# Four edits in a hybrid mixer and mixture-of-experts kernel: score blocks in pairs, logits in 32-token groups, an early subtraction, and a new home for the last down weights

## The chip, the cores and the metric

The kernel runs on one core of one Trainium2 chip. The metric is the time of one execution on the device, in microseconds (us); lower is better. All times below are of single executions or of medians of them.

## What is computed

One layer of a streaming encoder over 1024 prompt tokens and 64 sample tokens, all in float32. Cut to what matters:

```
h = rms_norm(x) * (1 + sc1) + sh1
hq, hf, hi, hog, gq, gk, gv, gog, glr, ga, gb = split(h @ w_in)      # one combined input projection
o_hg  = chunked gated linear attention, 4 heads of dk 128, decay from hf        # "hg" units
log_g = log_sigmoid(glr @ w_gk2 + b_gk) / 16                                     # low-rank gate
o_gla = chunked gated linear attention, 4 heads of dk 64, decay log_g           # "gla" units
merged = sigmoid(ga) * (o_hg @ w_br_a) + sigmoid(gb) * (o_gla @ w_br_b)
x = x + g1 * (merged @ w_out)
h = rms_norm(x) * (1 + sc2) + sh2
group = top1(h @ w_rg + b_rg); experts = top2 of 8 in the group (h @ w_re + b_re)   # 4 + 32 = 36 logits a token
x = x + g2 * sum over the two experts of wts * (silu(h @ w_gate[e]) * (h @ w_up[e])) @ w_down[e]
y = rms_norm(x)
```

There are 32 experts with gate and up weights of 1024 x 512 and down weights of 512 x 1024.

## The kernel before, in words

Matrix products in float32 precision are made as three products of operands split into a rounded half ("hi", the engine's fast float32 form) and a rest ("lo"): `split_matmul`, lines 149 to 151. The hi half is a copy to the rounded type (on GpSimd for the projection weights, line 737; on ScalarE for the experts' weights, line 2406). The lo half is a VectorE subtraction (line 1466 in the mixers, called `next_low`; line 2528 in the experts, called `low`). Small products (attention scores, outputs, transposes, logits) run as plain float32 matmuls, of which the trace records two passes each, every pass with a weight load of its own.

Each engine runs its own instruction list in program order; semaphores (`reach`, `wait_ge`) tie the lists together. So what comes late on one engine delays all that stands behind it on that engine.

**Mixers.** Six units run one after the other: two gla units of two heads (units 0 and 1), then four hg units of one head (units 2 to 5). The tokens are 9 tiles, eight of 128 and one of 64. In each unit TensorE first makes the unit's projections (`project`, three column chunks of 364, 364 and 360 tokens, 24 matmuls each), then runs the loop over `j`, one step for a tile and head: 18 steps in a gla unit, 9 in an hg unit. Step `j` makes the transposes of a new tile (`turn`, lines 804 and 806, when a tile begins), the score blocks of the next step (`scores(u, j + 1)`, line 820), projections of the next unit where some are due (`filled`; in a gla unit in every even step, in an hg unit in steps 0, 1, 3, 4, 6 and 7, in the last unit in steps 0 to 2), and the outputs of this step (`outputs(u, j)`, lines 847, 849 and 851). `scores` makes 28 products for a tile of 128: 24 of 32 tokens by 32 tokens, four blocks of 32 output partitions in turn, and 4 "far" ones; the array is used 32 output columns at a time. VectorE turns scores into a masked matrix with four instructions (`mask`, lines 1430 to 1440) and then advances the state (`advance`, line 1453). There are two score buffers: `scores(u, j)` waits until `mask` of `j - 2` has ended (`sc_ready`). `outputs(u, j)` needs `mask(j)`, the transposed tile that ScalarE copies (`keep_tok`, line 1139), and the state after `j - 1`.

**Start of unit 0.** After the channel products TensorE makes the low-rank product, its logits, the projection `q` and then `x0`, for which the lo half of the third weight block is needed (`w_lo_done` 3). VectorE makes that half in the loop over the seven levels, after the third level (`if l == 2: next_low()`). Before the levels it has `decay_log(0)`, `decay_bound(0)` and `decay_sum(0)`, which wait for three ScalarE steps. ScalarE's list holds the copy of `q` chunk 1 behind the exponentials of levels 0 and 1 (line 1080), and `project` of `x0` chunk 0 waits for that copy, too (`proj_kept`).

**Output projection and router.** For each tile `t` TensorE transposes `h2` (line 2058), makes half of the output projection of tile `t + 2`, then the logits of tile `t` (line 2069: for each of 8 channel blocks one matmul with 128 tokens as weights and 36 columns), then the other half. Tiles 7 and 8 have no projection behind them; there the routing of the last tiles is a chain of small VectorE instructions.

**Experts.** For each expert: `gate_up` (48 matmuls), transposes of the next expert's tokens, `down` of the expert before (24 matmuls), transposes of the hidden values. The raw weights arrive in a ring of eight 1 MB buffers. Behind the loop stands `down(NE - 1)` for the last expert. ScalarE's list at the last expert (31) is: the silu steps, `keep_y(30)` (copy of the result, which waits for `down(30)`), `hidden_high(31)`, the two halves of `high("d", 31)`. VectorE's is: `hidden(31)`, `hidden_low(31)`, the two halves of `low("d", 31)`. The split down weights go to `d_hi` and `d_lo`, which are in use until `down(30)` has ended. `down` starts when `hidden_low` and the first `low("d")` have ended.

Of the kernel before, what the change touches and what calls it, by code (L numbers as in the profile page):

```python
# [27 lines left out]
F32 = mybir.dt.float32  # L28
# [463 lines left out]
def mixers(nc, a, h, h_hi, h_lo, m_hi, m_lo, merged, ident, mod_d, mix_d, gate_d, outs, consts, ahead):  # L492
# [66 lines left out]
    with Stage(nc, "x") as s:  # L559
# [207 lines left out]
        def _(pe):  # L767
# [190 lines left out]
            for u in range(NU):  # L958
# [18 lines left out]
                for j in range(NS[u]):  # L977
                    if j + 1 < NS[u]:
                        if (j + 1) % SUB[u] == 0:
                            turn(u, (j + 1) // SUB[u])  # L980
                        scores(u, j + 1)
                    for (of, name), c in filled(u, j):
                        project(of, name, c)
                    outputs(u, j)
# [349 lines left out]
        def _(dve):  # L1334
# [202 lines left out]
            V.memset(p_far, 0.0).then_inc(far_zero, 1)  # L1537
            V.memset(state[:, :, :, :], 0.0).then_inc(state_zero, 1)
            decay_log(0)
            decay_bound(0)  # L1540
            decay_sum(0)
            for u in range(NU):
# [4 lines left out]
                for l in range(NL):  # L1547
                    level_diff(u, l)
                    if l == 2:
                        next_low()  # L1550
                    if l == 3:
                        ends_diff(u)
# [129 lines left out]
def out_router(nc, a, mod_d, x2_d, h2_d, m_hi, m_lo, ident, consts, route, early, ahead):  # L1682


    NTT = NT + 1
    eid, pos, wts, m_all = route["eid"], route["pos"], route["wts"], route["m_all"]
    with Stage(nc, "o") as s:
# [349 lines left out]
        def tensor(pe):  # L2037
# [23 lines left out]
            def logits(t):  # L2061
                n = TILES[t][1]
                reach(pe, hT_ready, t + 1)
                if t:
                    reach(pe, logits_kept, t)
                else:
                    pe.wait_ge(small_in, 64)
                for k in range(KD):
                    m = nc.tensor.matmul(p_l[0:n, 0:36], hT[:, k, 0:n], w_r[:, k, :], start=(k == 0), stop=(k == KD - 1))  # L2069
                m.then_inc(logits_done, 1)  # L2070
# [58 lines left out]
NE = 32  # L2129
# [33 lines left out]
def experts(nc, a, mod_d, x2_d, outs, consts, route, table_d, h2_d, y_d, ident, early, router):  # L2163
# [6 lines left out]
    with Stage(nc, "e") as s:  # L2170
# [82 lines left out]
        his, los, used = {"g": g_hi, "u": u_hi, "d": d_hi}, {"g": g_lo, "u": u_lo, "d": d_lo}, {"g": g_done, "u": u_done, "d": d_done}  # L2253

        def staged(part, e, half):

            return weight_rows(w[place[part, e, half] % RING], part)
# [138 lines left out]
        def _(act):  # L2396
            router.scalar(act)

            def high(part, e, halves=(0, 1)):

                for half in halves:
                    i = place[part, e, half]
                    reach(act, w_in[i % RING], 16 * (i // RING + 1))
                    if e and half == 0:
                        reach(act, used[part], e)
                    nc.scalar.activation(his[part][:, half_rows(part, half), :], staged(part, e, half), ACT.Copy).then_inc(hi_done[part], 1)  # L2406

# [36 lines left out]
            for e in range(NE):  # L2444
# [5 lines left out]
                if e:  # L2450
                    keep_y(e - 1)
                hidden_high(e)
                high("d", e)
            keep_y(NE - 1)
# [50 lines left out]
        def _(dve):  # L2505
# [17 lines left out]
            def low(part, e, halves=(0, 1)):  # L2523

                for half in halves:
                    rows = half_rows(part, half)
                    reach(dve, hi_done[part], 2 * e + half + 1)
                    V.tensor_tensor(los[part][:, rows, :], staged(part, e, half), his[part][:, rows, :].bitcast(F32),  # L2528
                                    ALU.subtract).then_inc(lo_done[part], 1)
# [72 lines left out]
            for e in range(NE):  # L2602
                hidden(e)
                if e + 1 < NE:
                    low("g", e + 1, (1,))
                    x_low(e + 1)
                    low("u", e + 1)
                hidden_low(e)
                low("d", e)
            n = number(dve)  # L2610
# [54 lines left out]
        def _(pe):  # L2665
# [33 lines left out]
            def down(e):  # L2699
# [9 lines left out]
                m.then_inc(d_done, 1)  # L2709

            router.tensor(pe)
            pe.wait_ge(filled, 2)
# [3 lines left out]
            for e in range(NE):  # L2716
# [5 lines left out]
                turn_hidden(e)  # L2722
            down(NE - 1)
            n = number(pe)
# [132 lines left out]
```

## Time and profile before

| | us |
|---|---|
| median of 3 runs | 1673.09 (1672.48 to 1675.18) |
| the profiled execution, its own time | 1672.9 |
| span of its trace | 1670.8 |
| TensorE busy | 1561.6 (93%) |
| TensorE weight loads busy | 1368.7 (82%) |
| VectorE busy | 1196.5 (72%) |
| ScalarE busy | 921.7 (55%) |
| GpSimd busy | 298.3 (18%) |

"PE" is TensorE's matmuls, "PEld" its weight loads, "DVE" VectorE, "ACT" ScalarE, "POOL" GpSimd; L820 is line 820 of the kernel. A busy TensorE is not one at its peak: matmuls are pipelined and the recorded duration of one reaches over the start of the next. So what a matmul costs is read from the distance between starts, not from durations. "Granted clock" is the share of full clock that TensorE was given.

### The profile page before, as it was taken

Reading aid. Unit: us, or ns where it says so; the run is one execution under the profiler, and the core shown is the slowest. Engines: PE = TensorE matmul, PEld = TensorE weight load, DVE = VectorE, ACT = ScalarE, POOL = GpSimd, SP = SyncE. Lnnn points to the kernel's source line nnn. Section 1 sums busy time; section 2 is a strip of 40 time slices with the busy share of each in tenths; the row PEclk is TensorE's granted clock in tenths of the full one; section 3 lists DMA queues with packets and bytes.
Section 4 is the critical chain, followed back from the end, with each engine's and each line's share of the span. In section 5 each row is a group of like instructions: output and inputs, shape, how many; then the busy total and the mean of one; then the engine's idle time right before and its main releaser. Section 6 shows DMA issues by size and latency. Waiting matters only on the chain. (4 is left out here: it accounts for less than half of the span.)

```text
span 1670.8 us, 29394 instructions
## 1 busy us (share of the span) xinstructions
PE 1561.6 (93%) x12436; PEld 1368.7 (82%) x12436; DVE 1196.5 (72%) x1537; ACT 921.7 (55%) x1094; POOL 298.3 (18%) x203
## 2 busy tenths in 40 slices
PE   5999999999999999998998995999999999999956
PEld 4899899999889989897997874788888888888842
DVE  5743583368466675758565467999999999999937
ACT  5542444336353463633112223888888888888832
POOL 2310020002010010102000001132344342232230
PEclk9999999999999999998999996999999999999988
DMA  9121022111324152324446338999999999999965
GB/s 332 49 78 34 23 69 93 40 42 43 118 74 150 58 189 89 96 96 139 152 159 220 118 115 311 341 373 386 392 383 394 386 380 388 383 381 396 373 221 227
DMA packets 129660, 346.07 MB, mean 207 GB/s; under 512 B 16464, under 2 KB 72504, under 8 KB 103864
## 3 DMA queue, kind: packets, MB, share of 16 engines
q1 hardware_dynamic: 113704, 312.29, 51.7%
q0 software_dynamic: 9824, 17.88, 2.8%
q10 hardware_dynamic: 6000, 13.99, 2.2%
q8 instruction: 100, 1.64, 0.4%
q14 instruction: 32, 0.26, 0.0%
HBM read 316.04 MB, written 43.81 MB: 215 GB/s over the span
## 5 line engine op out<-in xcount | busy, mean ns | idle before, releaser
L149 PE MATMUL wo_psum_m<-h_hi,x_w_hi 128*128 128x364 f32 (+1 forms) x1184 | 404.4, 342 | 9.7 <-DVE x_w_lo L1466 2.9
L151 PE MATMUL wo_psum_m<-h_hi,x_w_lo 128*128 128x364 f32 (+1 forms) x1184 | 390.4, 330 | 0.0
L150 PE MATMUL wo_psum_m<-h_lo,x_w_hi 128*128 128x364 f32 (+1 forms) x1184 | 390.4, 330 | 0.0
L149 PEld LDWEIGHTS wo_psum_m<-h_hi,x_w_hi 128*128 128x128 f32 x1184 | 223.7, 189 | 25.1 <-issue 12.8
L150 PEld LDWEIGHTS wo_psum_m<-h_lo,x_w_hi 128*128 128x128 f32 x1184 | 224.0, 189 | 2.5
L151 PEld LDWEIGHTS wo_psum_m<-h_hi,x_w_lo 128*128 128x128 f32 x1184 | 223.8, 189 | 0.0
L737 POOL CAST x_w_hi<-x_w 128x1024 fp32r<-128x1024 f32 x44 | 70.1, 1593 | 617.7 <-PE wo_psum_m L151 597.4
L2315 POOL DMA_INDIRECT scratch_y<-e_y,all_tbl x32 | 74.2, 2320 | 372.8 <-ACT e_y L2439 372.8
L1466 DVE TENSOR_TENSOR x_w_lo<-x_w,x_w_hi 128x1024 fp32r<-128x1024 f32 x52 | 65.2, 1253 | 92.5 <-POOL x_w_hi L737 61.7
L149 PE MATMUL e_psum_y<-e_d_hi,e_hid_hi 128*128 128x512 f32 x256 | 103.1, 403 | 5.3 <-DVE e_d_lo L2528 5.3
L149 PE MATMUL e_psum_g<-e_g_hi,e_x_hi 128*128 128x512 f32 x256 | 104.9, 410 | 3.2 <-DVE e_x_lo L2539 2.6
L151 PE MATMUL e_psum_g<-e_g_hi,e_x_lo 128*128 128x512 f32 x256 | 101.6, 397 | 0.0
L150 PE MATMUL e_psum_g<-e_g_lo,e_x_hi 128*128 128x512 f32 x256 | 101.4, 396 | 0.0
L151 PE MATMUL e_psum_y<-e_d_hi,e_hid_lo 128*128 128x512 f32 x256 | 100.3, 392 | 0.0
L150 PE MATMUL e_psum_y<-e_d_lo,e_hid_hi 128*128 128x512 f32 x256 | 100.2, 392 | 0.0
L151 PE MATMUL e_psum_u<-e_u_hi,e_x_lo 128*128 128x512 f32 x256 | 99.8, 390 | 0.0
L149 PE MATMUL e_psum_u<-e_u_hi,e_x_hi 128*128 128x512 f32 x256 | 99.6, 389 | 0.0
L150 PE MATMUL e_psum_u<-e_u_lo,e_x_hi 128*128 128x512 f32 x256 | 99.6, 389 | 0.0
L1035 ACT ACTIVATE x_x<-wo_psum_m 128x364 f32<-128x364 f32 (+1 forms) x48 | 22.5, 469 | 121.7 <-PE wo_psum_m L151 121.6
L1430 DVE TENSOR_TENSOR x_diag<-wo_psum_m,all_shapes 128x192 f32<-128x192 f32 (+1 forms) x72 | 37.1, 516 | 68.0 <-PE wo_psum_m L820 67.4
L2528 DVE TENSOR_TENSOR e_g_lo<-mg_ring_hi,e_g_hi 128x2048 fp32r<-128x2048 f32 x34 | 77.7, 2289 | 9.7 <-ACT e_g_hi L2406 9.5
L2528 DVE TENSOR_TENSOR e_d_lo<-mg_ring_lo,e_d_hi 128x2048 fp32r<-128x2048 f32 x34 | 76.2, 2284 | 1.1 <-ACT e_d_hi L2406 1.1
(380 smaller groups left out, 3521.6 us busy)
## 6 DMA issues: line engine op xcount, KB each, us to landing
mg_ring_hi<-in_w_e_gate SPq DMA_DIRECT2D x34, 1024.0 KB, 9.8
mg_ring_lo<-in_w_e_down SPq DMA_DIRECT2D x34, 1024.0 KB, 8.3
mg_ring_hi<-in_w_e_up SPq DMA_DIRECT2D x32, 1024.0 KB, 8.8
mg_ring_lo<-in_w_e_up SPq DMA_DIRECT2D x32, 1024.0 KB, 8.7
mg_ring_lo<-in_w_e_gate SPq DMA_DIRECT2D x30, 1024.0 KB, 9.9
mg_ring_hi<-in_w_e_down SPq DMA_DIRECT2D x30, 1024.0 KB, 8.1
x_w<-in_w_in SPq DMA_DIRECT2D x44, 512.0 KB, 3.9
scratch_gate<-x_x ACTq DMA_DIRECT2D x16, 544.0 KB, 3.3
```

The source lines that it names most:

```text
L149: nc.tensor.matmul(out, lhs[0], rhs[0], start=start, stop=False)
L150: nc.tensor.matmul(out, lhs[0], rhs[1], start=False, stop=False)
L151: return nc.tensor.matmul(out, lhs[1], rhs[0], start=False, stop=stop)
L737: nc.gpsimd.tensor_copy(w_hi[:, n % 2], w[:, n % 2]).then_inc(w_hi_done, 1)
L1035: nc.scalar.activation(dst[:, c0:c0 + n], bank[:, 0:n], ACT.Copy).then_inc(proj_kept, 1)
L1430: V.tensor_tensor(diag[0:n, j % 2].rearrange("p t l -> p l t"), p_diag[0:n, j % 2].rearrange("p (l t) -> p l t", t=SB), masks[0:n], ALU.mu ...
L1466: V.tensor_tensor(w_lo[:, n % 2], w[:, n % 2], w_hi[:, n % 2].bitcast(F32), ALU.subtract).then_inc(w_lo_done, 1)
L2315: nc.gpsimd.indirect_dma_start(out=y_d, out_offset=bass.IndirectOffsetOnAxis(ap=tbl[:, e:e + 1], axis=0), in_=y[:, e % 2, :], in_offset=No ...
L2528: V.tensor_tensor(los[part][:, rows, :], staged(part, e, half), his[part][:, rows, :].bitcast(F32), ALU.subtract).then_inc(lo_done[part], 1)
```

## The change

It does four things.

1. In the loop over `j`, the score blocks of steps `j + 1` and `j + 2` are both issued in even steps, and none in odd steps. Nothing is added or removed.
2. Each logits matmul becomes four (two for the tile of 64 tokens), each for 32 tokens, written to 32 output partitions.
3. In unit 0 the third `next_low()` stands ahead of `decay_log(0)` instead of behind the third level. (It is the lo half of a weight block; the low-rank product itself isn't moved.)
4. The last expert's down weights are split into the buffers of the gate weights. ScalarE's and VectorE's lists at expert 31 are reordered: first half of the down weights, hidden values, second half. `down(31)` becomes `last_down`, which issues the same 48 products in another order: all hi x hi first, then hidden hi with the lo of the first half, then hidden lo with all hi, then hidden hi with the lo of the second half.

```diff
@@ mixers, TensorE, loop over j
                     if j + 1 < NS[u]:
                         if (j + 1) % SUB[u] == 0:
                             turn(u, (j + 1) // SUB[u])
-                        scores(u, j + 1)
+                    for ahead_ in (1, 2):
+                        if j % 2 == 0 and j + ahead_ < NS[u]:
+                            scores(u, j + ahead_)
                     for (of, name), c in filled(u, j):
                         project(of, name, c)
                     outputs(u, j)
@@ mixers, VectorE
             V.memset(state[:, :, :, :], 0.0).then_inc(state_zero, 1)
+            next_low()
             decay_log(0)
...
                     level_diff(u, l)
-                    if l == 2:
+                    if l == 2 and u:
                         next_low()
@@ router, TensorE
                 for k in range(KD):
-                    m = nc.tensor.matmul(p_l[0:n, 0:36], hT[:, k, 0:n], w_r[:, k, :], start=(k == 0), stop=(k == KD - 1))
+                    for b0 in range(0, n, SPAN):
+                        m = nc.tensor.matmul(p_l[b0:b0 + SPAN, 0:36], hT[:, k, b0:b0 + SPAN], w_r[:, k, :],
+                                             start=(k == 0), stop=(k == KD - 1))
@@ experts, where the split halves go
+        def split_into(part, e):
+
+            if part == "d" and e == NE - 1:
+                return g_hi[:, :, :].rearrange("p (f h) c -> p f (h c)", f=KF), g_lo[:, :, :].rearrange("p (f h) c -> p f (h c)", f=KF)
+            return his[part], los[part]
@@ experts, ScalarE
-                    if e and half == 0:
+                    if part == "d" and e == NE - 1:
+                        reach(act, g_done, NE)
+                    elif e and half == 0:
                         reach(act, used[part], e)
...
                 if e:
                     keep_y(e - 1)
-                hidden_high(e)
-                high("d", e)
+                if e + 1 < NE:
+                    hidden_high(e)
+                    high("d", e)
+            high("d", NE - 1, (0,))
+            hidden_high(NE - 1)
+            high("d", NE - 1, (1,))
             keep_y(NE - 1)
@@ experts, VectorE
-                hidden_low(e)
-                low("d", e)
+                if e + 1 < NE:
+                    hidden_low(e)
+                    low("d", e)
+            low("d", NE - 1, (0,))
+            hidden_low(NE - 1)
+            low("d", NE - 1, (1,))
@@ experts, TensorE
+            def last_down():
+
+                e = NE - 1
+                hi, lo = split_into("d", e)
+                halves = [range(half * KF // 2, (half + 1) * KF // 2) for half in range(2)]
+                reach(pe, y_kept, e)
+                reach(pe, h_hi_done, e + 1)
+                for half, fs in enumerate(halves):
+                    reach(pe, hi_done["d"], 2 * e + half + 1)
+                    for c in range(0, D, HALF):
+                        for f in fs:
+                            nc.tensor.matmul(p_y[0:N, c:c + HALF], hid_hi[:, f, :], hi[:, f, c:c + HALF], start=(f == 0), stop=False)
+                reach(pe, lo_done["d"], 2 * e + 1)
...
-            down(NE - 1)
+            last_down()
```

## Rows read from the trace of the kernel before

**Rows 1.** Busy time by stage: window, length, PE, PEld, DVE, ACT, POOL, clock, DMA, GB/s.
```profile
320.00:360.00 40.00, 40.00 (x816) 36.16 (x815) 28.48 (x67) 15.27 (x32) 2.09 (x2) 1.00 0.11 29
...
920.00:960.00 40.00, 40.00 (x214) 34.07 (x213) 17.39 (x24) 7.07 (x13) 0.00 (x0) 1.00 0.30 111
...
1400.00:1440.00 40.00, 40.00 (x190) 33.51 (x189) 38.29 (x26) 35.83 (x29) 9.84 (x4) 1.00 1.00 388
```

**Rows 2.** Timeline, start of unit 0: start, length, engine, line, [idle before, releaser].
```profile
59.47 1.04 POOL L737 CAST x_w_hi<-x_w 128x1024 fp32r<-128x1024 f32 x1 [2.28 <-PE wo_psum_m L151]
...
68.47 1.29 DVE L1339 SCALAR_TENSOR_TENSOR x_t<-x_b,x_t 128x1088 f32<-128x1088 f32 x1 [7.28 <-ACT x_t L1049]
...
77.11 0.46 ACT L1033 ACTIVATE x_q<-wo_psum_m 128x364 f32<-128x364 f32 x1
...
77.24 2.06 DVE L1466 TENSOR_TENSOR x_w_lo<-x_w,x_w_hi 128x1024 fp32r<-128x1024 f32 x1
...
79.44 0.41 PE L149 MATMUL wo_psum_m<-h_hi,x_w_hi 128*128 128x364 f32 x1 [2.88 <-DVE x_w_lo L1466]
```

**Rows 3.** Busy time behind the stall of rows 2; columns as in rows 1.
```profile
79.40:83.50 4.10, 4.06 (x15) 4.09 (x16) 4.10 (x7) 1.83 (x3) 0.00 (x0) 0.58 0.47 128
```

**Rows 4.** Timeline, TensorE, one score block between a transpose and a projection.
```profile
556.15 0.27 PE L806 MATMUL x_psum_tok<-all_ident,x_v 128*128 128x128 f32 x1
556.36 0.27 PE L820 MATMUL wo_psum_m<-x_q,x_k 128*32 128x32 f32 x8
556.44 0.68 PE L820 MATMUL wo_psum_m<-x_lev 128*32 128x32 f32 x48
557.05 0.43 PE L149 MATMUL wo_psum_m<-h_hi,x_w_hi 128*128 128x364 f32 x1
```

**Rows 5.** Timeline, step 0 of units 1 and 2: mask 0 and score block 1.
```profile
313.17 0.52 DVE L1430 TENSOR_TENSOR x_diag<-wo_psum_m,all_shapes 128x192 f32<-128x192 f32 x1 [1.60 <-PE wo_psum_m L820]
...
313.63 0.67 PE L820 MATMUL wo_psum_m<-x_lev 64*32 64x32 f32 x48
...
314.44 0.29 DVE L1440 TENSOR_TENSOR x_sc<-x_sc,wo_psum_m 128x128 f32<-128x128 f32 x1
...
437.81 0.64 PE L820 MATMUL wo_psum_m<-x_lev 128*32 128x32 f32 x43
...
439.47 0.29 DVE L1440 TENSOR_TENSOR x_sc<-x_sc,wo_psum_m 128x128 f32<-128x128 f32 x1
```

**Rows 6.** Timeline, TensorE, unit 3: the transpose of step 6, and outputs behind outputs.
```profile
564.38 0.33 PE L804 MATMUL x_psum_tok<-all_ident,x_ke 128*128 128x128 f32 x1 [0.62 <-ACT x_tok L1139]
...
576.59 0.41 PE L847 MATMUL x_psum_o<-x_qe,x_state 128*128 128x64 f32 x2 [0.59 <-issue]
```

**Rows 7.** Timeline, router: the logits of one tile, what follows, and of the last tile.
```profile
990.48 1.87 PE L2069 MATMUL o_psum_l<-o_w_r,o_hT 128*128 128x36 f32 x16
...
992.18 0.43 PE L149 MATMUL wo_psum_m<-x_out,mg_hi 128*64 128x512 f32 x1
...
1010.84 0.19 DVE L1900 TENSOR_TENSOR wo_ring<-o_psum_l,o_b_r 64x36 f32<-64x36 f32 x1 [0.90 <-PE o_psum_l L2069]
```

**Rows 8.** Timeline, last expert, from the end of down(30) to the last product.
```profile
1600.13 1.02 ACT L2439 ACTIVATE e_y<-e_psum_y 128x1024 f32<-128x1024 f32 x1 [7.25 <-PE e_psum_y L151]
1601.05 0.59 ACT L2433 ACTIVATE e_hid_hi<-e_psum_h 128x512 fp32r<-128x512 f32 x1
...
1603.32 1.91 ACT L2406 ACTIVATE e_d_hi<-mg_ring_lo 128x2048 fp32r<-128x2048 f32 x1
...
1605.67 2.29 DVE L2528 TENSOR_TENSOR e_d_lo<-mg_ring_lo,e_d_hi 128x2048 fp32r<-128x2048 f32 x1
1605.91 0.77 PE L149 MATMUL e_psum_y<-e_d_hi,e_hid_hi 128*128 128x512 f32 x1 [5.35 <-DVE e_d_lo L2528]
...
1612.42 0.39 PE L150 MATMUL e_psum_y<-e_d_lo,e_hid_hi 128*128 128x512 f32 x1
1612.65 0.39 PE L151 MATMUL e_psum_y<-e_d_hi,e_hid_lo 128*128 128x512 f32 x1
```

More of the change, by code:

```diff
@@ L1682, in out_router @@
 def out_router(nc, a, mod_d, x2_d, h2_d, m_hi, m_lo, ident, consts, route, early, ahead):
-    NTT = NT + 1
+    NTT, SPAN = NT + 1, 32
     eid, pos, wts, m_all = route["eid"], route["pos"], route["wts"], route["m_all"]
@@ L2403, in high @@
                     reach(act, w_in[i % RING], 16 * (i // RING + 1))
-                    if e and half == 0:
+                    if part == "d" and e == NE - 1:
+                        reach(act, g_done, NE)
+                    elif e and half == 0:
                         reach(act, used[part], e)
-                    nc.scalar.activation(his[part][:, half_rows(part, half), :], staged(part, e, half), ACT.Copy).then_inc(hi_done[part], 1)
+                    nc.scalar.activation(split_into(part, e)[0][:, half_rows(part, half), :], staged(part, e, half), ACT.Copy).then_inc(hi_done[part], 1)
             def x_high(e):
@@ L2527, in low @@
                     reach(dve, hi_done[part], 2 * e + half + 1)
-                    V.tensor_tensor(los[part][:, rows, :], staged(part, e, half), his[part][:, rows, :].bitcast(F32),
+                    if part == "d" and e == NE - 1:
+                        dve.wait_ge(g_done, NE)
+                    hi, lo = split_into(part, e)
+                    V.tensor_tensor(lo[:, rows, :], staged(part, e, half), hi[:, rows, :].bitcast(F32),
                                     ALU.subtract).then_inc(lo_done[part], 1)
@@ L2709, in down @@
                 m.then_inc(d_done, 1)
+            def last_down():
[10 more added lines that the diff above has]
+                reach(pe, lo_done["d"], 2 * e + 1)
+                for c in range(0, D, HALF):
+                    for f in halves[0]:
+                        nc.tensor.matmul(p_y[0:N, c:c + HALF], hid_hi[:, f, :], lo[:, f, c:c + HALF], start=False, stop=False)
+                reach(pe, h_lo_done, e + 1)
+                for c in range(0, D, HALF):
+                    for f in range(KF):
+                        nc.tensor.matmul(p_y[0:N, c:c + HALF], hid_lo[:, f, :], hi[:, f, c:c + HALF], start=False, stop=False)
+                reach(pe, lo_done["d"], 2 * e + 2)
+                for c in range(0, D, HALF):
+                    for f in halves[1]:
+                        m = nc.tensor.matmul(p_y[0:N, c:c + HALF], hid_hi[:, f, :], lo[:, f, c:c + HALF], start=False, stop=(f == KF - 1))
+                m.then_inc(d_done, 1)
             router.tensor(pe)
```

## The prediction, made before the changed kernel was run

> **What bounds the kernel now.** I read busy time by stage first. In three windows far apart, in the mixers' loop, in the router and in the experts, TensorE is busy for all of 40 us at full granted clock [rows 1]. So in these stages an instruction taken out of TensorE's list comes off the time, unless a wait for another engine takes its place. In the experts the DMA engines stand at 1.00 as well, but the change takes no TensorE work out there except at the end. Second, the list of TensorE's idle times over 0.25 us: about 50, nearly all at the start of the kernel, at the turns between units, in the last routing and at the end. Two of them are touched by the change: 2.88 us at 79.44 for a lo half [rows 2] and 5.35 us at 1605.91 for another [rows 8]. Third, the timeline around score blocks, logits and these two waits, from which I take distances between starts.
>
> **Logits in 32-token groups.** Now: 16 weight-load-and-matmul pairs (8 matmuls, two passes each) from 990.48 to the next kind of work at 992.18 take 1.70 us, 0.106 us a pair [rows 7]. After: 64 pairs with 32 weight columns. The nearest rows are the scores, with the same 32 output columns in four groups in turn: 48 pairs last 0.68 us, of which about 0.20 is the last one's own duration, so (0.68 - 0.20) / 47 = 10.2 ns a pair [rows 4]. 64 pairs are 0.66 us. But such a block has fixed costs at both ends: its first pair comes 0.21 us after a transpose that, at full width, takes 0.11 (0.10 extra), the next work starts 0.11 us later than the pace gives (0.69 us from 556.36 to 557.05 for 56 pairs, 0.57 at the pace), and the first projection matmul lasts 0.43 us against 0.33 of its kind (0.10 more) [rows 4]. Sum 0.31 us. New block 0.97 us, gain 0.73 us for a tile. TensorE is the bound for tiles 0 to 6 (7 x 0.73 = 5.1). Tile 7's logits lie before a wait of TensorE for VectorE: nothing. Tile 8's: VectorE idles 0.90 us for them [rows 7]; it has two groups instead of four, so half the pairs at, I assume, twice the distance, the same 0.66 us and 0.31; 0.7 to 0.9 us go, I take the 0.9 of the idle time. What is late next there is VectorE's own list. Logits: **-6.0 us**. Bounds: 0.106 us a pair (no concurrency at all) would be 6.8 us a block, +5.4 a tile; a pace of 7 ns gives -0.2 more a tile. I take the scores' pace, since width, groups and kind are the same; 36 columns against 32 are the only difference.
>
> The Trainium skill, page "TensorE: Matmul & The Clock Gate", section "Wait — 56ns, not 53.3ns?", speaks against this edit: starts of matmuls never come closer than about 25 ns. By it 64 pairs would take 1.6 us and the block 1.9 us, more than now. The trace disagrees: 10.2 ns a pair in the scores [rows 4]. The skill's "TensorEngine Tiling (Array Packing)", section "Tiling Modes", says that changing the tiling mode drains the engine, while tiles of one mode run in parallel; the extra 0.31 us at the ends of a score block are what such a drain would look like.
>
> **Score blocks in pairs.** The block itself stays. Of the two blocks of a pair, one pair of ends goes: 0.31 us [rows 4]. Pairs: 8 in each gla unit (17 blocks behind the first), 4 in each hg unit, 32 in all: 32 x 0.31 = 9.9 us. Against that stand new waits:
> - The second block of a pair waits for `mask(j)`, whose scores came a pair earlier. In steps from 2 on the mask is made under the projections of the step before; costed at nothing, by 4 us of projections against two masks of 1.56 us (313.17 to 314.73) [rows 5]. In step 0 there is no such cover. Unit 1: block 1 ends at 313.63 + 0.68 - 0.1 = 314.2, mask 0 at 314.73, so block 2 starts about 0.6 us late [rows 5]; unit 0 has the same form, 0.6. Unit 2: block 1 ends at about 438.35, mask 0 at 439.76, since VectorE had a lo half in front of it: 1.5 us [rows 5]. Units 3 to 5: the transpose of tile 1 already waits for ScalarE, and mask 0 ends in that time: 0.
> - In hg units, outputs of odd steps without projections now stand directly behind outputs of the step before and need its state. One such place is in the trace: 0.59 us of idle time at 576.59 [rows 6]. With the transpose (0.22) between, 0.37 us for step 5 of each hg unit.
> - In step 6 the transpose waits for ScalarE until 564.38, 0.62 us [rows 6]. ScalarE comes no earlier, while TensorE has a block and its ends less in front of this wait: of the gain, 0.9 us less the 0.37 (counted once) is lost, 0.9 in all with it for units 2, 3 and 4.
>
> Sum: units 0 and 1 8 x 0.31 - 0.6 = 1.9 each; unit 2 1.24 - 1.5 - 0.9 = -1.2; units 3 and 4 1.24 - 0.9 = 0.35 each; unit 5, whose steps 3 to 8 have no projections, 1.24 - 0.37 = 0.9. **-4.2 us**. Bounds: -9.9 (no new wait) and +3 (a wait of 0.4 us in each pair).
>
> **The lo half ahead of the decay.** The half takes VectorE 2.06 us at 77.24, and TensorE waits 2.88 us for it [rows 2]. Its source is ready at 59.47 + 1.04 = 60.5, and VectorE is idle for 7.28 us before 68.47 [rows 2]: there it is free, its cover is that idle time, and without it it would cost 1.3 to 2.1. Late next is ScalarE's copy of `q` chunk 1, 77.11 + 0.46 = 77.57 [rows 2], whose releasers (levels 0 and 1) don't move. So TensorE starts at about 77.65 instead of 79.44: 1.8 us. After the stall the granted clock was 0.58 for 4.1 us, 15 matmuls in 4.1 us; at full clock these are 2.5 [rows 3]. The clock was full before this stall. With 1.1 us of idle time left I expect that it stays so, as it did through the 0.62 us at 564.38 [rows 6]; at 1.1 us no row here shows it. 1.6 us. **-3.4 us**; bounds -1.8 (the clock falls all the same) and -4.5.
>
> **The last down weights.** The gate buffers are free early, but ScalarE's `keep_y(30)` stands in front of the first split and ends with `down(30)`, at 1600.13 + 1.02 [rows 8]. So the split starts no earlier than the list allows: the new home buys nothing by itself, the order does. After: first hi half from 1601.05 (where `hidden_high` was), 1.80 us; `hidden_high` 1602.85 to 1603.44; second hi half to 1605.2. TensorE starts at 1603.5 instead of 1605.91. It then idled for 3.0 us and will run at half clock for about 3 us, as now: from 1605.91 to 1612.65 stand 23 distances, which are 5.3 us at the 0.23 us of the last two rows, 6.74 in fact [rows 8]. Four products to 1605.2, four to about 1606.8, the lo of half one (VectorE, ready at 1605.3) to 1607.7, eight with the hidden lo (ready at 1605.9) to 1609.5, the last four (second lo half, 2.3 us behind the hidden lo, ready at 1608.2) to 1610.4 against 1612.9 now. **-2.5 us**; bounds -0.5 (half clock throughout) and -3.5. The copy, the scatter and the final sums move with it; the second lo half, formerly under the first products, is now covered by sixteen.
>
> **Sum.** 6.0 + 4.2 + 3.4 + 2.5 = 16.1 us. The profiled execution took 1672.9 us (span 1670.8), 0.2 below the median of 1673.1. 1673.1 - 16.1 = **1657.0 us**.
>
> **Rivals.**
> - *The logits gain nothing.* Groups of 36 columns that accumulate over eight blocks might not overlap as single score blocks do, and stay near 27 ns a pair (1.70 / 64) plus 0.31: +0.3 x 7 instead of -6.0: 1665. For it: no row shows accumulating groups; against it: the pace of the scores. This is also where the skill's 25 ns floor leads. Chance 0.10.
> - *The pairs gain nothing*, their ends being taken up by waits for masks, ScalarE or states: 1661. For it: units 2 to 4 as worked out. 0.17.
> - *The other side: each pair waits for a mask.* Were VectorE always a block behind, the second block would wait a whole mask (1.6 us) in each of 32 pairs: 51 us - 9.9 + what the other edits give, -11.9: 1702. It decides from a mean wait of (9.9 + 11.9) / 32 = 0.68 us. Against it: 4 us of projections in most steps. 0.02.
> - *It doesn't do what it says at the end:* the gate buffers free nothing, and if the half clock lasts longer, the last expert gives 0.5 instead of 2.5: 1659. 0.10.
> - *More is hidden in the ends of blocks* than I count (the scores' own pace, tile 7, unit 5): 1652. 0.16.
> - The forecast, 1654 to 1660: 0.45.
>
> **Range and chances.** 1651 to 1665 holds all but the outer parts of these. A measurement of this kernel can tell about 0.2% (3.3 us) from no change. Faster by more 0.96, within 0.01, slower 0.03.
>
> **What the profile will show.** Right: L1466 in the idle time before 68.47, the first `x0` matmul at about 77.65 and full clock behind it; 64 passes of L2069 in about 0.8 us a tile, and 5 us less from 902 to 998; double score blocks of 1.3 us and 40 instead of 72 groups; the wait of TensorE for VectorE's masks in step 0 of units 0 to 2 and hardly elsewhere; the first down product of the last expert about 3 us behind the transposes. Wrong: a distance of over 20 ns between logits passes; waits for L1440 of more than 0.7 us a pair; a granted clock below 1 in the router or the loops.

## The result and the profile after

The changed kernel took 1660.64 us in the median of 4 runs (1659.88 to 1663.04) against 1672.78 for the kernel before on the same chip: ratio 0.9927, 95% interval 0.9914 to 0.9940, or -12.1 us. The forecast was 1657.0 (1651 to 1665). A second measurement of the same kernel gave 1659.96 (5 runs) against 1673.66: 0.9916, 0.9903 to 0.9930, -14.0 us by the ratio. The profiled execution of the first took 1659.88 us, span 1658.0, so 12.8 of span are to be placed. The page, busy times:

```profile
PE 1541.9 (93%) x12836; PEld 1352.8 (82%) x12836; DVE 1197.3 (72%) x1537; ACT 921.3 (56%) x1094; POOL 301.5 (18%) x203
```

Windows of the changed kernel, with the columns of rows 1. The three long ones are those of [rows 1], the last lies behind the wait of [rows 2] and answers [rows 3]:

```profile
320.00:360.00 40.00, 39.59 (x789) 36.99 (x791) 27.12 (x63) 14.93 (x31) 2.09 (x2) 1.00 0.10 29
920.00:960.00 40.00, 40.00 (x369) 32.61 (x368) 17.13 (x24) 8.03 (x15) 0.00 (x0) 1.00 0.36 133
1400.00:1440.00 40.00, 40.00 (x190) 33.48 (x189) 37.56 (x25) 35.27 (x31) 11.67 (x5) 1.00 1.00 384
79.00:83.00 4.00, 4.00 (x26) 4.00 (x25) 4.00 (x7) 2.02 (x4) 0.11 (x1) 1.00 0.00 0
```

TensorE is still full in all three stages. The mixers' loop has 0.41 us of idle time that it did not have: one wait for a mask. Behind the `x0` wait the clock is 1.00 instead of 0.58.

**Start.** Timeline of TensorE, the two waits that are left there:

```profile
78.50 0.43 PE L149 MATMUL wo_psum_m<-h_hi,x_w_hi 128*128 128x364 f32 x1 [1.04 <-ACT x_q L1035]
...
91.10 0.40 PE L149 MATMUL wo_psum_m<-h_hi,x_w_hi 128*128 128x364 f32 x1 [0.37 <-DVE x_w_lo L1468]
```

This execution had come to its first `q` products 0.89 us later than the one of before. (So had those of all the other kernels below, by 0.4 to 1.5 us: the profile of before was early there.) Less that, the first `x0` matmul is at 77.61; forecast 77.65, and the releaser is ScalarE's copy of `q`, as said. The second row is a wait that the forecast does not have.

**Score blocks.** Timeline of TensorE: step 0 of unit 0, block 1 and the start of block 2, the first mask wait of unit 2, and two rows of unit 3 that answer [rows 6]:

```profile
152.34 0.26 PE L820 MATMUL wo_psum_m<-x_q,x_k 64*32 64x32 f32 x8
152.42 0.67 PE L820 MATMUL wo_psum_m<-x_lev 64*32 64x32 f32 x48
153.57 0.27 PE L820 MATMUL wo_psum_m<-x_q,x_k 64*32 64x32 f32 x8 [0.48 <-DVE x_sc L1442]
...
434.37 0.27 PE L820 MATMUL wo_psum_m<-x_q,x_k 128*32 128x32 f32 x8 [1.35 <-DVE x_sc L1442]
...
558.13 0.46 PE L847 MATMUL x_psum_o<-x_qe,x_state 128*128 128x128 f32 x2 [0.27 <-issue]
...
560.03 0.33 PE L804 MATMUL x_psum_tok<-all_ident,x_ke 128*128 128x128 f32 x1 [1.00 <-ACT x_tok L1141]
```

The waits stand where they were expected: 0.48 for mask 0 in unit 0 (forecast 0.6), 1.35 in unit 2 (1.5), 0.27 for a state (0.37), and ScalarE in step 6 with 1.00 where it was 0.62.

**Router.** Logits of tile 7 and of tile 8, and the first gather of the experts with the product that waits for it:

```profile
989.57 0.77 PE L2073 MATMUL o_psum_l<-o_w_r,o_hT 128*32 128x36 f32 x64 [1.11 <-ACT o_hT L1836]
...
997.49 1.18 PE L2073 MATMUL o_psum_l<-o_w_r,o_hT 128*32 128x36 f32 x32 [0.32 <-ACT o_hT L1836]
...
1010.45 1.19 POOL L2320 DMA_INDIRECT e_xg<-scratch_h,all_src x1 [18.32 <-DVE all_src L2031]
...
1016.13 1.97 PE L2696 MATMUL e_psum_x<-all_ident,e_xg 128*128 128x128 f32 x8 [4.63 <-DMA e_xg<-scratch_h,all_src]
```

64 pairs take 0.77 us where 16 took 1.87 [rows 7]: (0.77 - 0.20) / 63 = 9.0 ns a pair. Tile 8 (the second row) runs at a granted clock of 0.50, before and after.

**Last expert.** The rows that answer [rows 8]:

```profile
1589.23 1.02 ACT L2452 ACTIVATE e_y<-e_psum_y 128x1024 f32<-128x1024 f32 x1 [7.25 <-PE e_psum_y L151]
1590.15 1.90 ACT L2419 ACTIVATE e_g_hi<-mg_ring_lo 128x2048 fp32r<-128x2048 f32 x1
1591.95 0.59 ACT L2446 ACTIVATE e_hid_hi<-e_psum_h 128x512 fp32r<-128x512 f32 x1
...
1592.64 3.61 PE L2746 MATMUL e_psum_y<-e_g_hi,e_hid_hi 128*128 128x512 f32 x8 [2.98 <-ACT e_hid_hi L2446]
...
1598.83 1.07 PE L2758 MATMUL e_psum_y<-e_g_lo,e_hid_hi 128*128 128x512 f32 x4
```

The wait is 2.98 us instead of 5.35, and the first eight products take 3.61 us: they run at half clock. The product of the last expert has 24 matmuls in all, before and after (8, 4, 8 and 4 here), not the 48 that the section on the change names.

**Where the time went, by stage.** Change in the length of each stretch against the profiled execution of before, in us, from the starts of the same instruction in both timelines. The columns are kernels of the next part; a star marks a fall of the granted clock in that kernel (0.57 to 0.66 over 4 us) at about 65, 255 or 433 us, where the kernel before kept 1.00. At 255 and 433 it stands behind a wait of 2.1 and 1.35 us; at 65 us TensorE had come from the low-rank logits (L775) with no wait over 0.2 us.

```
                         changed  again  pairs  logits  low   last  early  combined
start to first scores     -1.85  -1.92* -1.06* -0.74* -2.09  +0.47 -2.01  -2.23
units 0 and 1             -3.58  -3.77  -2.17* +1.58* -0.09  +0.13 -2.19* -3.73
unit 2                    +1.14  +2.56* +1.17  -0.06  +0.01  -0.08 +1.10   0.00
units 3 and 4             -0.72  -0.76  -0.69  -0.05  +0.09  -0.05 -0.75  -0.82
unit 5, way to router     +0.35  -1.74  -0.75  +0.10  -2.35  -0.73 -1.46  -0.80
router, to last ranks     -7.39  -7.32  -0.03  -7.43  -0.04  -0.01 -7.33  -6.96
last routing, experts 0,1 +1.16  +0.98  -0.14  +1.02  -0.77  +0.49 +1.01  +0.98
experts 2 to 30           -0.01   0.00  -0.01   0.00  -0.01   0.00  0.00   0.00
last expert               -2.24  -2.28  -0.08  +0.57  -0.09  -2.28 -5.57  -5.57
final sums                +0.34  +0.25  -0.14  +0.31  -0.16  -0.14 -0.70  -0.57
```

### The profile page after: what moved, and what is told of

Its sections match the earlier page's. It is cut to its first block and busy times, and to the rows that moved or that the text cites. A ratio compares the mean times of both kernels' runs of the same rounds, so it can differ in the third digit from the quotient of the medians.

```text
span 1658.0 us, 30197 instructions
## 1 busy us (share of the span) xinstructions
PE 1541.9 (93%) x12836; PEld 1352.8 (82%) x12836; DVE 1197.3 (72%) x1537; ACT 921.3 (56%) x1094; POOL 301.5 (18%) x203
## 5 line engine op out<-in xcount | busy, mean ns | idle before, releaser
L149 PE MATMUL e_psum_y<-e_d_hi,e_hid_hi 128*128 128x512 f32 x248 | 99.1, 400 | 0.0
L151 PE MATMUL e_psum_y<-e_d_hi,e_hid_lo 128*128 128x512 f32 x248 | 96.7, 390 | 0.0
L150 PE MATMUL e_psum_y<-e_d_lo,e_hid_hi 128*128 128x512 f32 x248 | 96.7, 390 | 0.0
L2548 DVE TENSOR_TENSOR e_g_lo<-mg_ring_lo,e_g_hi 128x2048 fp32r<-128x2048 f32 x32 | 73.2, 2289 | 17.3 <-ACT e_g_hi L2419 17.0
L1455 DVE SCALAR_TENSOR_TENSOR x_state<-x_state,x_eb_last,x_psum_u 64x128 f32<-64x128 f32 (+1 forms) x72 | 24.9, 346 | 80.9 <-PE x_psum_u L851 80.3
```

Source lines behind the costliest of these rows:

```text
L149: nc.tensor.matmul(out, lhs[0], rhs[0], start=start, stop=False)
L150: nc.tensor.matmul(out, lhs[0], rhs[1], start=False, stop=False)
L151: return nc.tensor.matmul(out, lhs[1], rhs[0], start=False, stop=stop)
L1455: new = V.scalar_tensor_tensor(out=state[ch, to, s_, :], in0=state[ch, of, s_, :], scalar=eb_last[ch, u % 2, i:i + 1], in1=p_u[ch, s_ * DV ...
L2548: V.tensor_tensor(lo[:, rows, :], staged(part, e, half), hi[:, rows, :].bitcast(F32), ALU.subtract).then_inc(lo_done[part], 1)
```

## The experiments

The theory under test is the forecast's: TensorE's list is the bound, each edit's worth is what it takes out of that list less the waits it makes. The single edits come first, on one chip: 6 executions of the logits alone, 12 of each of the others, and 29 of the kernel before, with a median of 1673.51 us. Differences in us are worked out from the ratio. By the plain medians the four would be -7.8, -2.5, -2.4 and -3.1.

**Logits alone** (`logits_only`).

```diff
-    NTT = NT + 1
+    NTT, SPAN = NT + 1, 32
...
-                    m = nc.tensor.matmul(p_l[0:n, 0:36], hT[:, k, 0:n], w_r[:, k, :], start=(k == 0), stop=(k == KD - 1))
+                    for b0 in range(0, n, SPAN):
+                        m = nc.tensor.matmul(p_l[b0:b0 + SPAN, 0:36], hT[:, k, b0:b0 + SPAN], w_r[:, k, :],
+                                             start=(k == 0), stop=(k == KD - 1))
```

> Only the logits in 32-token groups. If the gain is TensorE's own time: 0.85 to 0.9 us a tile for tiles 0 to 6 and about 1.1 at tile 8, -7.3 us. If part of the 7.4 us lost between 902 and 1016 us came from the other edits: -6.0 or less, as predicted. If the first rows of the modulation still arrive late, that wait is unchanged here.

Measured: 1665.76 us, ratio 0.9961 (0.9947 to 0.9974), -6.5 us. The router stretch is 7.43 shorter, as in the changed kernel, and about 1 us comes back at the gather.

**Pairs alone** (`pairs_only`).

```diff
-                        scores(u, j + 1)
+                    for ahead_ in (1, 2):
+                        if j % 2 == 0 and j + ahead_ < NS[u]:
+                            scores(u, j + ahead_)
```

> Only the score blocks in pairs; all else as before. Theory of the prediction, mended by the trace of the changed kernel: each joined pair saves its two ends (0.31 us), new waits take part of it back; units 0 and 1 gain 2.2 and 1.4 us, unit 2 loses 1.1 (mask 0 is late), units 3 and 4 gain 0.4 each, unit 5 0.7: -3.9 us from the first score block to the end of unit 5. Rival: the new waits eat the ends, within 1 us of before. Rival: the joins give more and the end of the mixers hides it, -8 us up to unit 5.

Measured: 1671.03 us, ratio 0.9991 (0.9982 to 1.0001), -1.5 us and not told from nothing. In its profile unit 0 is 2.24 us shorter up to the wait ahead of its mean of squares (the changed kernel 2.22), and loses 1.51 of it behind that wait, where the clock fell (below). Unit 1 gives -1.4, unit 2 +1.17, units 3 and 4 -0.69. Up to the end of unit 5 that is -2.3 us, or -3.8 without the fall, for the -3.9 expected.

**The lo half alone** (`low_only`).

```diff
+            next_low()
...
-                    if l == 2:
+                    if l == 2 and u:
```

> Only the third lo half ahead of the decay. Wait for the x0 projection 2.88 -> 1.0 us, full granted clock behind it: -3.4 us at the first score block; of it about 0.4 is given back to a new wait for the lo half of the fourth block. At the end 0.5 us may be lost again where the rows of the modulation are awaited ahead of the router. Rival: the clock falls all the same, -1.8 us.

Measured: 1671.16 us, ratio 0.9991 (0.9983 to 1.0000), -1.5 us; the profile shows -2.7 between the `q` products and the first scores, 1.82 of it at the wait. At the first scores it is 2.09 us early where 3.4 was expected; 0.65 had been lost ahead of the `q` products.

**The last down weights alone** (`last_only`): the home in the gate buffers, the order of the two lists and the order of the last product.

```diff
+            if part == "d" and e == NE - 1:
+                return g_hi[:, :, :].rearrange("p (f h) c -> p f (h c)", f=KF), g_lo[:, :, :].rearrange("p (f h) c -> p f (h c)", f=KF)
...
+            high("d", NE - 1, (0,))
+            hidden_high(NE - 1)
+            high("d", NE - 1, (1,))
```

> Only the last expert: buffers, lists and the order of the products. -2.2 us between the transposes of the hidden values and the last copy; everything before is the same. Rival: the gate buffers allow the split ahead of the end of down(30), -4 us or more.

Measured: 1670.44 us, ratio 0.9983 (0.9972 to 0.9993), -2.8 us; -2.28 in the last expert. The four single edits come to -12.3 together (-15.7 by the medians), against -12.2 and -14.0 for all at once: no edit is seen to need or spoil another, to within the scatter of about 3 us.

**The order without the gate buffers** (`order_only`), one execution, 1672.02 for the kernel before beside it. The kernel above, with the new home taken back:

```diff
         def split_into(part, e):
-            if part == "d" and e == NE - 1:
-                return g_hi[:, :, :].rearrange("p (f h) c -> p f (h c)", f=KF), g_lo[:, :, :].rearrange("p (f h) c -> p f (h c)", f=KF)
             return his[part], los[part]
```

> The last expert as changed (lists and order of the products), but the down weights split into their old buffers. If the new home buys nothing, since the copy of y(30) stands in front: 2.2 us less than before between the hidden transposes and the last copy, as with the gate buffers. If the home matters, 1.5 us or more of this is gone.

Measured: 1671.57 us. The last expert is 2.27 us shorter, against 2.28 with the gate buffers. Timeline of this kernel:

```profile
1601.07 1.02 ACT L2443 ACTIVATE e_y<-e_psum_y 128x1024 f32<-128x1024 f32 x1 [7.25 <-PE e_psum_y L151]
1601.99 1.90 ACT L2410 ACTIVATE e_d_hi<-mg_ring_lo 128x2048 fp32r<-128x2048 f32 x1
...
1604.48 3.59 PE L2735 MATMUL e_psum_y<-e_d_hi,e_hid_hi 128*128 128x512 f32 x8 [2.98 <-ACT e_hid_hi L2437]
```

The same 2.98 us of wait into the old buffers: the new home adds nothing, and the whole gain of this edit is in the order. That is the order of the two lists and that of the products together: TensorE can start on hi x hi before any lo half is there only because `last_down` has these products first. No kernel had one without the other.

**The split really ahead** (`early_split`): the changed kernel, with ScalarE's two hi halves ahead of `keep_y(30)` and VectorE's lo halves ahead of the hidden lo. Only this makes use of the gate buffers: the first split starts at 1581.15, while `down(30)` still reads the old ones until about 1588.5.

```diff
+                if e + 1 == NE:
+                    high("d", e)
                 if e:
                     keep_y(e - 1)
+                hidden_high(e)
...
-            high("d", NE - 1, (0,))
-            hidden_high(NE - 1)
-            high("d", NE - 1, (1,))
```

> The changed kernel, with the high halves of the last down weights split ahead of the copy of the product of expert 30 in ScalarE's list, and both low halves ahead of the hidden rows' low half on VectorE: so the gate buffers' early freedom is used. Theory (the order of the lists held the split, the buffers did not): ScalarE has only the copy of the product and the hidden rows' high half behind the transposes, 1.0 + 0.6 us, so TensorE starts the last down product about 1.2 to 1.8 us after 1589.0 + 1.6, that is at 1590.9 instead of 1592.6, and the wait of 2.98 us becomes about 1.2; -1.8 us, and another -1.0 to -1.6 if the granted clock then does not fall behind it: ratio to the changed kernel 0.9980 to 0.9990. Rival (what bounds the end is the DMA of the last down weights or VectorE's low half): the start moves but a new wait of 1 to 2 us stands inside the product, and the gain is under 0.5 us.

Measured: 1655.68 us, ratio to the kernel before 0.9891 (0.9876 to 0.9906), and 4.3 us under the changed kernel beside it (1659.96). Timeline:

```profile
1581.15 3.71 ACT L2419 ACTIVATE e_g_hi<-mg_ring_lo 128x2048 fp32r<-128x2048 f32 x2
...
1589.42 0.59 ACT L2446 ACTIVATE e_hid_hi<-e_psum_h 128x512 fp32r<-128x512 f32 x1
...
1590.11 2.09 PE L2744 MATMUL e_psum_y<-e_g_hi,e_hid_hi 128*128 128x512 f32 x8 [1.18 <-ACT e_y L2452]
```

The windows of 3 us from the first product, the changed kernel first:

```profile
1592.60:1595.60 3.00, 2.96 (x7) 2.18 (x8) 3.00 (x3) 1.74 (x1) 0.00 (x0) 0.50 0.29 116
```

```profile
1590.10:1593.10 3.00, 2.99 (x13) 2.49 (x14) 0.64 (x1) 0.00 (x0) 2.68 (x5) 1.00 0.00 0
```

Both halves of the gain are seen: the wait falls from 2.98 to 1.18, and eight products take 2.09 us instead of 3.61, since the clock stays full. Behind the wait of 1.18 us it was 1.00 in both kernels that have it, and 0.50 behind 2.98 us in all four that have that. The last expert is 5.57 us shorter than before, 3.3 beyond the change, at the upper end of what was expected (1.7 to 3.3). Another 1.0 in the final sums was not expected. 0.7 of it is the scatter of the last rows: it lands 3.2 us behind its issue, as in every other kernel, but 3.9 in both profiles of the changed one. Why is open. The rival (a new wait inside the product) falls.

**The same, unit 2 not paired** (`combined`).

```diff
-                    for ahead_ in (1, 2):
-                        if j % 2 == 0 and j + ahead_ < NS[u]:
+                    for ahead_ in ((1,) if u == 2 else (1, 2) if j % 2 == 0 else ()):
+                        if j + ahead_ < NS[u]:
```

> As the kernel with the early split, but unit 2 keeps one score block a step (units 0, 1, 3, 4 and 5 stay paired). Theory: pairing costs unit 2 1.1 to 1.2 us (waits of 1.35 us for x_sc in step 0 and of 1.00 us for ScalarE in step 6), so the span from the start of unit 2 to the start of unit 3 comes back to what it was before, -1.15 us against the early split alone; about 1656.5 to 1658.5 us in all. Rival (the waits only move, as TensorE meets ScalarE's list later in the unit anyway): 0 to -0.3 us.

Measured: 1654.31 us, ratio 0.9882 (0.9867 to 0.9897), 1.4 under the kernel with the early split (within the scatter of single medians, but with its place): unit 2 is 0.00 us from its length before, where pairing cost +1.10. This is the fastest kernel of the study.

**The logits' groups one after the other** (`logits_serial`), one execution. The same 32-column pairs, all eight blocks of one group before the next group, instead of the groups in turn.

```diff
+                for b0 in range(0, n, 32):
+                    for k in range(KD):
+                        m = nc.tensor.matmul(p_l[b0:b0 + 32, 0:36], hT[:, k, b0:b0 + 32], w_r[:, k, :],
```

> The same 32-token logits products, but all eight channel blocks of one group of 32 tokens before the next group, so that neighbours use the same 32 output columns. If groups gain because different output columns overlap, the pace falls from 9 ns a pair to 25 ns or more, 1.6 us a tile or more, no gain against before. If the narrow weights alone make them fast, the pace stays near 10 ns and the gain stays.

**Two groups of 64** (`logits_64`), one execution: `SPAN` is 64.

> Logits in two groups of 64 tokens: 32 pairs a tile. With overlap and half the load width: 0.106 / 2 / 2 = 27 ns a pair, 0.85 us plus the ends, about half of the gain of four groups. With the narrow load alone: 53 ns, 1.7 us plus ends, no gain.

Measured: 1672.55 and 1672.11 us (1672.02 before). To the last tile's logits the router is 2.22 us longer with the groups one after the other and 4.00 shorter with two of 64. The logits of tile 7 and what follows, serial, then 64:

```profile
989.88 1.96 PE L2070 MATMUL o_psum_l<-o_w_r,o_hT 128*32 128x36 f32 x64
991.77 0.44 PE L149 MATMUL wo_psum_m<-x_out,mg_hi 128*64 128x512 f32 x1
```

```profile
989.43 1.13 PE L2070 MATMUL o_psum_l<-o_w_r,o_hT 128*64 128x36 f32 x32
990.49 0.45 PE L149 MATMUL wo_psum_m<-x_out,mg_hi 128*64 128x512 f32 x1
```

A pair takes (1.96 - 0.20) / 63 = 28 ns when its neighbour has the same group, and 9 ns in turn; 64 columns wide and in turn (1.13 - 0.23) / 31 = 29 ns; 128 wide 106 [rows 7]. So the narrower pair costs in proportion to its columns (106 to 28), which gains nothing for a whole tile, and all of the gain is in the turn-taking: 3.1 times for four groups. In turn, neighbours differ in two things, the columns of the array and the output that they add to; one after the other they share both. No kernel had the one without the other, so that it is the columns is likely but not shown. The 4.0 us of the 64 kernel didn't reach its end time, which is one execution and carries a fall of the clock worth 1.5 us in unit 0; as a time it decides nothing.

**Blocks cut in two** (`cut_blocks`), one execution. The kernel before, with the turn of the next tile put between the third and the fourth of the six groups of levels in its score block instead of ahead of it: the same instructions, and one more pair of ends in each such step.

```diff
+                    if between and i_ == 3:
+                        between()
...
-                        if (j + 1) % SUB[u] == 0:
-                            turn(u, (j + 1) // SUB[u])
-                        scores(u, j + 1)
+                        fresh = (j + 1) % SUB[u] == 0
+                        scores(u, j + 1, (lambda: turn(u, (j + 1) // SUB[u])) if fresh else None)
```

> The kernel before, with the transposes of a new tile put into the middle of the score block instead of ahead of it: 48 blocks are cut in two, nothing is added. If the ends of a block of 32-column products cost 0.31 us, 48 more of them are +13 to +15 us over the six units. If the idle time at the blocks comes from something else, for instance the first scores of a step, within 2 us of before.

Measured: 1678.45 us against 1672.02, +6.4, under half of the +13 to +15 expected. Single executions of the kernel before lie between 1669.1 and 1678.1, so the stretches say more than the time. Timeline of one cut block:

```profile
167.69 0.26 PE L820 MATMUL wo_psum_m<-x_q,x_k 64*32 64x32 f32 x8
167.77 0.31 PE L820 MATMUL wo_psum_m<-x_lev 64*32 64x32 f32 x16
168.01 0.33 PE L804 MATMUL x_psum_tok<-all_ident,x_ke 128*128 128x128 f32 x1
168.17 0.38 PE L806 MATMUL x_psum_tok<-all_ident,x_v 128*128 128x128 f32 x2
168.49 0.55 PE L820 MATMUL wo_psum_m<-x_lev 64*32 64x32 f32 x32
```

Units 0 and 1 are longer by 2.1 us each for 8 cuts, 0.26 us a cut; units 2 to 4 by 0.8 to 0.95 for 8, 0.11 a cut. In the first two TensorE is the bound and the ends cost about what the forecast took from [rows 4]; in the others most of it disappears in idle time that is there anyway (the wait for ScalarE of [rows 6]). So ends are real, and what they are worth depends on the wait behind them.

**The changed kernel again** (`after_again`), beside the two variants.

> The changed kernel once more, beside the two variants of it. Both theories: 1660.6 us in the median and a ratio of 0.9927 to the kernel before. What it tells apart is where the granted clock falls: if it falls in other places in each execution, the 4 us behind the wait ahead of the first mean of squares, the first x0 matmuls at 78.5 and expert 1 will not show the same levels as in the first profile of this kernel (1.00, 1.00 and 0.50 to 0.76); if the place follows from the program, they will.

Measured: 1659.96 us. Of the ten stretches six repeat to 0.1 us and two more to 0.2, but two do not: unit 2 is 1.4 us longer, and unit 5 with the way to the router 2.1 shorter. The place of the fall is not the same: this execution has one at 65 us (0.57) and one in unit 2, the first profile neither. The window of 4 us from 433, first profile and second:

```profile
433.00:437.00 4.00, 2.65 (x69) 2.54 (x68) 2.57 (x8) 0.00 (x0) 0.00 (x0) 1.00 0.56 152
```

```profile
433.00:437.00 4.00, 2.89 (x62) 2.72 (x63) 2.31 (x8) 0.00 (x0) 0.00 (x0) 0.65 0.52 139
```

The same program, the same wait of 1.35 us in it, and a granted clock of 1.00 and 0.65. So the second of the two theories, that the place follows from the program, falls.

## Why the prediction was right, point by point

- **The bound.** Right. Instructions taken out of TensorE's list came off the time in the mixers and in the router; no stage changed its bound (the last steps of unit 5, where TensorE waits for VectorE, never were TensorE's, see below), and experts 2 to 30 kept their length to 0.01 us.
- **Logits, -6.0.** The mechanism was right, the size too small: -7.4 to the last ranks. Tiles 0 to 6 gave 0.89 us each for 0.73, and another 0.4 came around tile 7, which had been put at nothing. The pace is 9.0 ns for the 10.2 of the scores, which makes 0.08 us of a tile's 0.16; the other 0.08 are ends that cost less than the scores' 0.31. Tile 8 gave 0.74, forecast 0.9. Before, it was

```profile
1008.81 1.92 PE L2069 MATMUL o_psum_l<-o_w_r,o_hT 128*64 128x36 f32 x16 [0.32 <-ACT o_hT L1833]
```

  Both run at a clock of 0.50: 108 ns a pair then, 30 ns now in two groups, where the forecast had taken 20 at full clock. **What the sum did not have:** the first gather behind the router. Its issue is 12.05 us earlier, its landing 11.2. Before, issue and landing:

```profile
1022.50 1.19 POOL L2309 DMA_INDIRECT e_xg<-scratch_h,all_src x1 [19.64 <-DVE all_src L2028]
...
1027.33 1.97 PE L2672 MATMUL e_psum_x<-all_ident,e_xg 128*128 128x128 f32 x8 [3.77 <-DMA e_xg<-scratch_h,all_src]
```

  That is 4.83 us, and 5.68 after. In the 2 us behind the issue of the second gather the DMA engines stand at 0.71 before and at 0.90 after:

```profile
1024.00:1026.00 2.00, 0.00 (x0) 0.00 (x0) 2.00 (x2) 0.00 (x0) 2.00 (x1) 0.50 0.71 248
```

```profile
1012.00:1014.00 2.00, 0.00 (x0) 0.00 (x0) 2.00 (x2) 0.00 (x0) 2.00 (x1) 0.50 0.90 342
```

  From the last ranks to the gathered rows all five kernels with the 32-token logits in turn are 0.8 to 1.1 us longer; the seven others are between 0.4 shorter and 0.5 longer. A shorter router brings the gather closer to the experts' weight transfers, which are still under way. That these slow the gather fits the rows; no kernel moved the transfers to test it. Net, the edit gave about -6.4 in the profile and -6.5 by the ratio, near the forecast's -6.0 by two errors of opposite sign: luck. The Trainium skill's floor of about 25 ns between starts of matmuls ("TensorE: Matmul & The Clock Gate", section "Wait — 56ns, not 53.3ns?") is not what the chip does with groups in turn: 9.0 ns. It is close to the 28 ns of `logits_serial`.
- **Pairs, -4.2.** Unit 0 gave 2.2 (1.9), unit 1 1.35 (1.9: it has two waits for masks, 0.48 and 0.41 us, where one was counted), unit 2 cost 1.14 (1.2), units 3 and 4 gave 0.36 each (0.35). Unit 5 was put at 0.9, "whose steps 3 to 8 have no projections", and this is the step that failed: its -0.73 is no gain, for `logits_only`, `low_only` and `last_only` show -1.05, -0.53 and -0.48 there without pairs. Without projections TensorE waits in steps 5 to 8 for VectorE's states and masks, so an end saved there need not be time saved. The outputs of steps 5 and 8, before and then after:

```profile
757.68 0.46 PE L847 MATMUL x_psum_o<-x_qe,x_state 128*128 128x128 f32 x2 [1.12 <-DVE x_state L1453]
...
766.52 0.41 PE L847 MATMUL x_psum_o<-x_qe,x_state 128*128 128x64 f32 x2 [1.19 <-DVE x_sc L1440]
```

```profile
752.32 0.46 PE L847 MATMUL x_psum_o<-x_qe,x_state 128*128 128x128 f32 x2 [1.01 <-DVE x_state L1455]
...
760.78 0.41 PE L847 MATMUL x_psum_o<-x_qe,x_state 128*128 128x64 f32 x2 [0.64 <-DVE x_sc L1442]
```

  Up to step 5 all five kernels with pairs are 0.35 us ahead, and none of the others is. Behind it TensorE idles 2.6 to 4.1 us up to step 8 with pairs and 2.3 to 3.3 without, and the clock falls at another place from profile to profile (its mean was 0.88 over the 14 us from 755 in the kernel before). So up to step 8 the kernels with pairs lie between 0.7 us shorter and 0.3 longer, those without between 1.9 shorter and even. Without unit 5 the profile gives about -3.2, the ratio of `pairs_only` -1.5 with an interval from -3.0 to +0.2. The ends, 0.31 each, were right: `cut_blocks` has 0.26.
- **The lo half, -3.4.** The place (-1.83 for 1.8) and the full clock behind it were right. That the clock can stay full behind 1.1 us of idle time stood in the trace of before, in rows that the prediction did not use: it was 1.00 in the 4 us behind waits of 2.13 us at 259.10 and of 1.15 at 437.32. The clock was put at -1.6 and gave -0.9: full speed brings TensorE to the wait of 0.37 us at 91.10, for the next lo half, and the rest of the difference is not placed. More important is that the stall's price is not fixed. From the `q` products to the first scores, of the eight kernels without this edit (the kernel before among them) four are within 0.1 us of the length before, with a fall behind the wait; four are 1.4 to 1.6 shorter. In three of these the clock had fallen already at 65 us, and the half speed ran down the wait; window of 4 us from 65, `pairs_only`, then the kernel before:

```profile
65.00:69.00 4.00, 4.00 (x17) 4.00 (x17) 0.14 (x1) 3.73 (x4) 0.00 (x0) 0.59 0.01 4
```

```profile
65.00:69.00 4.00, 4.00 (x26) 4.00 (x25) 0.53 (x1) 3.71 (x5) 0.00 (x0) 1.00 0.00 0
```

  In the fourth, `cut_blocks`, TensorE waited 2.87 us for the same lo half and the clock stayed full, against 0.58 behind 2.88 us in [rows 3]:

```profile
79.95 0.40 PE L149 MATMUL wo_psum_m<-h_hi,x_w_hi 128*128 128x364 f32 x1 [2.87 <-DVE x_w_lo L1467]
```

```profile
79.95:84.05 4.10, 4.10 (x25) 4.10 (x26) 4.10 (x7) 1.88 (x3) 0.00 (x0) 1.00 0.47 128
```

  In all five kernels with the edit the stretch is 2.6 to 2.8 shorter, also where the clock fell at 65 us (`after_again`, 0.57). So the edit is worth 2.7 us against an execution that loses the clock behind the wait and 1.2 against one that doesn't. The ratio of `low_only`, -1.5, agrees with a mix.
- **Last down weights, -2.5.** Right in place and size: -2.24. TensorE started 3.61 us behind the transposes (forecast 3.57), at half clock, as said. That the gate buffers by themselves buy nothing was right too (`order_only`); that the split could start no earlier than the list allowed was so by the list alone: once it stands further ahead in the list, `early_split` is 4.3 us faster than the changed kernel.
- **Sum.** 16.1 us forecast, 12.8 in the profile, 12.1 and 14.0 by the two ratios. The 3.3 us between forecast and profile: the logits 1.4 more, but 0.85 lost at the gather; the pairs 1.0 less; the start 1.55 less, 0.89 of it lost ahead of the `q` products; the last expert 0.3 less; and 1.0 of small losses on the way to the router, in the first experts and in the tail, which the other kernels show with either sign. That the total still lies within the range is in part luck: the start, the pairs and the way to the router fell short, and the logits gave more than forecast. Of the rivals, "pairs gain nothing" came nearest in time (1661), but not by its mechanism: units 0 and 1 do gain. "Logits gain nothing" and "each pair waits for a mask" are refuted by rows at 989.57 and 152.34.

## What to carry to other kernels

Narrow matmuls in different column groups of the array, issued in turn, were 3 times as fast as the same matmuls group by group; for a whole tile it is the turn-taking that pays, not the narrow group. A buffer that is free early is worth nothing while the instruction that fills it stands behind a waiting one in its engine's list, so move both, and look whether the wait that is left is short enough for the clock to stay up: at the last expert this gave 1.5 us more. Before an edit is made for all units alike, price each unit by what waits behind it: here four gained, one (unit 5, where TensorE waits for VectorE) neither gained nor lost, and one lost 1.1 us.

## What the runs showed of the hardware that was not expected

The granted clock does not follow from the program alone. Ahead of the mean of squares of unit 0 TensorE waits 2.1 us in every one of the kernels. Here the changed kernel and the one with the early split, which have the same code up to there, row and window each:

```profile
255.03 0.85 PE L860 MATMUL x_psum_tok<-x_t,x_mean 128*128 128x364 f32 x2 [2.12 <-ACT x_t L1153]
```

```profile
255.00:259.00 4.00, 3.97 (x22) 3.77 (x23) 1.74 (x2) 1.81 (x3) 0.00 (x0) 1.00 0.83 270
```

```profile
254.85 0.85 PE L860 MATMUL x_psum_tok<-x_t,x_mean 128*128 128x364 f32 x2 [2.14 <-ACT x_t L1153]
```

```profile
255.00:259.00 4.00, 4.00 (x15) 3.77 (x16) 1.57 (x2) 1.64 (x3) 0.00 (x0) 0.61 0.82 270
```

22 matmuls against 15 in the same 4 us, and 1.5 us on the stretch of units 0 and 1. Of the thirteen profiles with that of before, four show the fall at this place, four at 65 us (behind no wait over 0.2 us) and one at 433 us, in kernels that share the code up to there with kernels that don't; and one kept the full clock behind the 2.87 us at 79.95. A fall in the loop costs 1.4 to 1.5 us, as much as the pairs or the lo half bring in a median. At this size two executions can't be compared by their spans: it takes stretch by stretch with the clock beside each, or medians of many.
